# The GLA gate matmul of a hybrid decoder layer: two token halves in two 32-row groups of the array

## The reference, cut to what matters

```python
z = xn @ p["w_in"] + p["b_in"]               # all mixers' inputs, split by columns
# GLA, T = 528 tokens, 4 heads, GLA_DK = 128
g = jax.nn.log_sigmoid((a_lr @ p["w_gla_a2"] + p["b_gla_a"]).astype(jnp.float32)) / GLA_TAU
g = g.reshape(B, T, GLA_H, GLA_DK)
# per chunk of 64 tokens:
G = jnp.cumsum(g, axis=2)
decay = jnp.exp(jnp.where(causal[None, None, :, :, None], G[:, :, :, None, :] - G[:, :, None, :, :], -jnp.inf))
A = jnp.einsum("bhtk,bhtsk,bhsk->bhts", q, decay, k)
o = jnp.einsum("bhtk,bhkv->bhtv", q * jnp.exp(G), S) + jnp.einsum("bhts,bhsv->bhtv", A, v)
# afterwards
mix = sigmoid(gate_a) * y_a + sigmoid(gate_b) * y_b + sigmoid(gate_c) * y_c
h = h + rms_norm(mix @ p["w_out"], p["g_post_mix"])
```

## Time and profile before

| | us |
|---|---|
| median of 3 timed runs | 1294.49 (1294.04 to 1294.63) |
| the profiled execution's own time | 1293.61 |
| its span, first to last instruction | 1291.9 |
| mean granted TensorE clock | 0.999 |

### The profile page before, as it was taken

The page is one execution under the profiler, slowest core; times in us unless marked ns, Lnnn a source line. Parts: engine busy times, 40 slices in busy tenths (PEclk is TensorE's granted clock), DMA queues, the critical chain, the costliest instruction groups (busy, mean ns, idle before and its releaser), DMA issues.

```text
span 1291.9 us, 17528 instructions
## 1 busy us (share of the span) xinstructions
PE 1280.8 (99%) x6604; PEld 1042.3 (81%) x6604; DVE 602.7 (47%) x1086; ACT 398.0 (31%) x822; POOL 768.2 (59%) x919
## 2 busy tenths in 40 slices
PE   9999999999999999999999999999999999999998
PEld 8866887677898889777898987787888888888886
DVE  4248788642275766734545563241611111333434
ACT  5243555533013323434032334311511111212322
POOL 8737430125654543656864446786576676788882
PEclk9999999999999999999999999999999999999999
DMA  7745200223321222222343333443233333222221
GB/s 193 229 153 172 81 2 26 67 65 91 98 76 56 66 58 58 66 82 66 99 105 91 82 99 98 143 135 96 63 103 92 89 97 114 87 93 98 98 82 66
DMA packets 168445, 120.59 MB, mean 93 GB/s; under 512 B 12394, under 2 KB 146640, under 8 KB 168361
## 3 DMA queue, kind: packets, MB, share of 16 engines
q1 hardware_dynamic: 161654, 108.32, 28.9%
q10 hardware_dynamic: 6706, 11.15, 2.7%
HBM read 115.20 MB, written 9.62 MB: 97 GB/s over the span
## 4 chain that ended last, share of the span: by engine, by line
PE 98%; DVE 1%; ACT 1%; issue 0%; ACTq 0%
PE GP L1827 45%; PE GP L1862 9%; PE PA L1862 9%; PE GP L1842 7%; PE GP L1824 7%; PE PA L2026 3%; PE GP L2088 3%; PE PA L2230 2%; PE PA L2125 2%; PE PA L2063 1%; PE PA L2137 1%; PE GP L1907 1%; PE PA L1996 1%; PE PA L2222 1%; PE GP L2301 1%; PE PA L2027 1%
## 5 line engine op out<-in xcount | busy, mean ns | idle before, releaser
L622 POOL TENSOR_TENSOR wlo<-wraw,whi 128x256 fp32r<-128x256 f32 x712 | 566.1, 826 | 14.8
L618 POOL TENSOR_SCALAR whi<-wraw 128x1024 fp32r<-128x1024 f32 x178 | 194.9, 1095 | 484.0 <-PE GP L1827 248.6
L1827 PE MATMUL GP<-xh,whi 128*128 128x512 f32 x352 | 147.1, 418 | 0.0
L1827 PE MATMUL GP<-xh,wlo 128*128 128x512 f32 x352 | 139.1, 395 | 0.0
L1827 PE MATMUL GP<-xl,whi 128*128 128x512 f32 x352 | 138.8, 394 | 0.0
L1770 DVE TENSOR_TENSOR ul<-U,uh 128x512 fp32r<-128x512 f32 x64 | 65.0, 1051 | 109.7 <-ACT uh L1152 109.7
L1827 PE MATMUL GP<-nh,whi 128*128 128x512 f32 x240 | 95.1, 396 | 0.0
L1827 PE MATMUL GP<-nl,whi 128*128 128x512 f32 x240 | 95.1, 396 | 0.0
L1827 PE MATMUL GP<-nh,wlo 128*128 128x512 f32 x240 | 95.1, 396 | 0.0
L1774 DVE SCALAR_TENSOR_TENSOR U<-GP,rrow 128x512 f32<-128x512 f32 x32 | 22.1, 692 | 141.7 <-PE GP L1827 140.3
L1827 PEld LDWEIGHTS GP<-xh,whi 128*128 128x128 f32 x352 | 66.2, 188 | 17.3 <-issue 2.9
(11 more groups left out here) (406 smaller groups left out, 2789.9 us busy)
## 6 DMA issues: line engine op xcount, KB each, us to landing
wraw<-in_w_in SPq DMA_DIRECT2D x75, 512.0 KB, 3.8
wraw<-in_w_up SPq DMA_DIRECT2D x32, 512.0 KB, 4.0
wraw<-in_w_down SPq DMA_DIRECT2D x32, 512.0 KB, 3.5
line_rows<-bias_line SPq DMA_DIRECT2D x8, 655.0 KB, 5.2
table<-line_rows SPq DMA_DIRECT2D x4, 1024.0 KB, 5.2
wraw<-in_w_br_dsa SPq DMA_DIRECT2D x8, 512.0 KB, 4.0
wraw<-in_w_br_gla SPq DMA_DIRECT2D x8, 512.0 KB, 3.9
wraw<-in_w_br_ml SPq DMA_DIRECT2D x8, 512.0 KB, 4.1
```

The lines of the kernel that those rows point to most:

```text
L618: nc.gpsimd.tensor_scalar(hi, src, 1.0, 1.0, ALU.mult, ALU.mult).then_inc(hi_done, 1)
L622: part = nc.gpsimd.tensor_tensor(lo[:, at:to], src[:, at:to], hi[:, at:to].bitcast(FP32), ALU.subtract)
L1827: ins = mm(ps[0:t.m, 0:SEQ], wt[:, s0, w], av, start=st, stop=sp_)
```

## The change

The gate's product of each head is still two multiplies over 264 tokens each, but each now uses 32 rows of the array instead of 128: the first half of the tokens (b = 0) on partitions 32 to 63, the second (b = 1) on partitions 0 to 31. For that

- a second DMA puts the weight on partitions 0 to 15 of `a2` as well (L838 of the changed kernel), and the three DMAs raise `ld_a` to 48 instead of 32;
- DVE copies the second half of the gate rows (32 partitions x 264) from partitions 32 to 63 of `small` down to partitions 0 to 31 (L1375), after it has waited for `gla_c` = 1, and counts up `gla_c` to 2;
- PE waits, before `gq0`, for `ld_a` = 48 and for `gla_c` = 2.

```diff
@@ ACT @@
             act.wait_ge(a2_zero, 1)
-            act.dma_start(a2[32:32 + META, :], a["w_gla_a2"][0]).then_inc(ld_a, 16)
+            for r in (2 * META, 0):
+                act.dma_start(a2[r:r + META, :], a["w_gla_a2"][0]).then_inc(ld_a, 16)
@@ DVE @@
             nc.vector.memset(KHt[:, :], 0.0).then_inc(gla_c, 1)
             dve.wait_ge(gla_c, 1)
-            dve.wait_ge(ld_a, 32)
+            nc.vector.tensor_copy(small[0:2 * META, HALF:ALL], small[2 * META:4 * META, HALF:ALL]).then_inc(gla_c, 1)
+            dve.wait_ge(ld_a, 48)
@@ PE, gemm() @@
                     for b in range(2):
-                        ins = mm(ps[:, b * SEQ:b * SEQ + HALF], a2[:, h * DK:(h + 1) * DK], small[:, b * HALF:(b + 1) * HALF],
+                        r = slice(2 * META * (1 - b), 2 * META * (2 - b))
+                        ins = mm(ps[:, b * SEQ:b * SEQ + HALF], a2[r, h * DK:(h + 1) * DK], small[r, b * HALF:(b + 1) * HALF],
                                  start=True, stop=True)
@@ PE, between yb7 and gq0 @@
-            pe.wait_ge(ld_a, 32)
+            pe.wait_ge(ld_a, 48)
+            pe.wait_ge(gla_c, 2)
```

## The result

| | before | changed |
|---|---|---|
| median of the runs, us | 1294.49 | 1301.62 (1300.86 to 1302.01, 4 runs) |
| profiled execution's own time | 1293.61 | 1301.98 |
| its span | 1291.9 | 1300.2 |
| mean granted clock | 0.999 | 0.997 |

The ratio is 1.0055, with a 95% interval of 1.0039 to 1.0071: 7.1 us slower (5.0 to 9.2). The kernel is slower by more than its measurement is uncertain.

The account below looks back on a forecast made before the run. The prediction took PE to bound the kernel: wait +6.0, clock +1.5 and gates -0.8 make +6.7 us, so 1301.2 on the median of 1294.49. The range holding 8 in 10 was 1299.0 to 1303.4.

Parts of the forecast that it names:

- What bounds the kernel: PE, busy 1280.8 of 1291.9 us, sets the end; no slack there can absorb a delay at 341 us.
- The third rival: Later waits of PE shrink by as much as the delay at `gq0`, giving 1293.7 us; chance 0.03.
- The wait: Before `gq0`, PE waits for DVE's COPY behind five MEMSETs: start 5.93 us later, term +6.0 us (5.7 to 6.5).
- The straight line through two copies: DVE's COPY of 264 elements, interpolated between copies of 32 (0.18 us) and 384 (0.54): 0.42 us.
- The 0.1 on top: At `gq0`, first weights can't load while an earlier multiply runs: 0.1 us more in the wait's term.
- The clock: After the pause before `gq0`, PE runs at half pace for 3.4 us: +1.5 us (0 to 3.1).
- The first rival: The clock stays up through the pause before `gq0`: +5.2 us in all, 1299.7 us; chance 0.12.
- The gates: Gate products of four heads run as overlapping pairs: 0.27 us saved for `gg0`, 0.17 each for three others, -0.8 us.
- The second rival: The row groups of the gate products don't overlap: gates +0.8 us, time 1302.8 us; chance 0.08.
- The sum: Wait, clock and gates over the whole kernel: 6.0 + 1.5 - 0.8 = +6.7 us, 1301.2 on the median.

Follow-up runs that it names:

- e5: The changed kernel with DVE's COPY moved ahead of the five MEMSETs, right behind the product with `yb7`: 1297.07 us, ratio 1.0018.
- e2: The kernel before with only a wait added: PE waits for the last of the five MEMSETs before `gq0`: 1301.45 us, ratio 1.0055.
- e7: The changed kernel with 25 small multiplies on PE ahead of the wait, to fill it: 1299.74 us, ratio 1.0045.
- e4: The kernel before with both gate multiplies of a head on the same 32 rows, no copy and no new wait: 1296.76 us, ratio 1.0018.
- e6: The changed kernel with DVE's COPY between the third and fourth of the five MEMSETs: 1299.69 us, ratio 1.0047.
- e3: The changed kernel with 50 small multiplies on PE ahead of the wait: 1306.11 us, ratio 1.0091.
- e9: The kernel of e5 with nine small multiplies where PE waits ahead of the MLP: 1295.67 us, ratio 1.0011 against the kernel before.

## Why the prediction was right

**What bounds the kernel: right.** PE's list is the time, and a delay on PE at 341 us was not given back: the stages add up to the span's difference (8.31 of 8.3). The third rival (the wait is given back) is out.

**The wait: right, a little too long.** Forecast 5.93 to the start of `gq0`, measured 5.82. The COPY took 0.28 and not 0.42, and from its end to `gq0` it was 0.10 (346.88 to 346.98) and not 0.05. The straight line through two copies gave half too much because the earlier trace rows mix a copy made beside a working POOL (the one of 384 elements) with copies made while it was idle: the same COPY took 0.28 here, while POOL was idle, and 0.53 in e5, ahead of the MEMSETs, with POOL at work. That it is POOL which makes the difference fits all nine runs that have the COPY, but no run isolates it:

```profile
342.15 0.53 DVE L1369 COPY small<-small 32x264 f32<-32x264 f32 x1
```

The 0.1 on top, for `gq0`'s first weight load, is there, but behind the start of `gq0`: its second multiply comes 0.31 after the first in e5, at full clock (342.78 and 343.09), and 0.57 instead of 0.42 in the change.

**The clock: the step is right, the size was too small for this execution.** Forecast 1.5, from 3.4 us at half pace; measured 2.75 in the profiled execution (5.87 us at half pace, each losing 0.45), 1.73 in e2's, 1.9 by medians (e7 against the change). The range of 0 to 3.1 held it. Its price per microsecond, 0.45, was right: 2.6 of 2.75. The length was taken from a row that doesn't show the clock: PE's pace at the start was half, but the earlier trace rows have the granted clock at 1.00 there. The first rival (the clock stays up) is out by the windows of the change. e7 shows what such a kernel takes, 1299.74; that the rival's time, 1299.7, agrees so closely is in part luck, as its wait was 0.2 too long and its gates' gain 0.5 too large.

**The gates: the sign is right, the size is not.** Forecast -0.8, measured -0.26. The step that failed is "0.75 instead of 1.02, a gain of 0.27 for `gg0`". In the trace of before, the product behind `gg0` already waits for DVE's evacuation of the keys (L1391 there); this row of PE's weight loads, which the prediction didn't look up, says so:

```profile
353.54 0.19 PEld L1842 LDWEIGHTS GP<-whi,xh 128*128 128x128 f32 x1 [0.39 <-DVE kh L1391]
```

The evacuation doesn't depend on `gg0`, and behind a shorter `gg0` PE only waits longer for it: 0.22 us of PE's own wait now. From the last pair of `gk0`'s multiplies to `gv0A` it is 353.54 - 352.28 = 1.26 before and 362.17 - 360.91 = 1.26 after: no gain. For the other heads I had said 0.17 each. The timeline of before around `gg1`:

```profile
378.19 1.00 PE L2125 MATMUL PA<-QL,KL 128*128 128x64 f32 x8
379.02 1.11 PE L1847 MATMUL GP<-small,a 128*128 128x264 f32 x4
379.97 1.00 PE L2125 MATMUL PA<-QL,KL 128*128 128x64 f32 x8
```

The gate itself went from 0.95 (to the start of the next group) to 0.64, a gain of 0.31. But the first group before it takes 0.93 instead of 0.83, so from level group to level group it is 1.57 instead of 1.78, and the second group grew from 1.00 to 1.10. Its first weight load started 0.22 ahead of its first multiply before, and starts with it in the changed kernel:

```profile
379.75 1.08 PEld L2125 LDWEIGHTS PA<-QL,KL 128*128 128x128 f32 x8
```

```profile
388.38 0.97 PEld L2129 LDWEIGHTS PA<-QL,KL 128*128 128x128 f32 x8 [0.34 <-issue]
```

That leaves 0.1 net, and three times 0.1 is about the 0.26. The second rival, no overlap, is out: e4 shows what that looks like. Its remark that 32-row groups appear nowhere in the trace was a misreading: L1896 has four such multiplies at 9.6 to 10.6 us, 32 rows by 16 columns.

The Trainium skill's rule in "TensorEngine Tiling (Array Packing)", section "Tiling Modes", that a change of mode drains the engine, agrees with e4: with the drain and no overlap the gates lose 1.17 us. Its rule in "TensorE: Matmul & The Clock Gate", section "Why this matters for your kernels", to avoid idle gaps, agrees with e2 and e7.

**The sum.** 6.0 + 1.5 - 0.8 = 6.7 was forecast, 5.8 + 2.75 - 0.26 = 8.3 was measured in the profiled execution and 7.1 by medians. The errors of the clock and the gates add up in one direction and that of the wait goes against them. So the mechanism was right, but that 1301.2 came within 0.4 of the median of 1301.62 is in part luck: the clock's share is smaller in the medians than in the profiled execution, and the executions alone differ by more than that. The range's upper end doesn't follow from its terms, 1294.49 + 6.4 + 3.1 - 0.8 = 1303.2 and not 1303.4; nothing hangs on it.

## What to carry to other kernels

Before a wait is added on the engine that sets the end, list what stands in front of the signal on the other engine's queue: here a copy of 0.28 us cost 5.8, because five MEMSETs that nobody waited for stood ahead of it, and moving it up 48 us made it free. Price a pause of PE at more than its length, since the clock can fall in it. And a block on PE gains only if the next one is free to start: look at who ends the wait of the instruction behind it.

## What the runs showed that I had not expected

- The clock can fall after PE has gone on: in e6 PE restarted at 345.84 and the clock was still at 1.00 up to 346.40 and 0.50 from 346.55.
- Waits as short as 1.4 and 0.5 us, with 0.66 us of transposes between them, were followed by a fall in the profiled executions of e4 and e5 (the rows at 931 and 930 us) and of e3 (at 940), and not in those of the other kernels that have them, before and the change among them. Ahead of the first wait stand more transposes, so in e5 PE did nothing but eight instructions of transposes from 926.76 to 929.92. From the first multiply of the up projection to the first of the down projection e5 took 1109.54 - 923.82 = 185.72 us and e9, with the waits filled, 1108.57 - 924.25 = 184.32; the median went down by 1.4, too. So an edit with a small effect of its own can seem to cost more by a fall of the clock elsewhere: e4's stage grew by 1.17 and its median moved by 2.4. What decides whether the clock falls there is not shown; that PE reaches the pause at another time is a guess.
- A change of array mode costs time at both ends: a gate block on 32 rows without overlap lost about 0.3 us (e4), and with its pair side by side kept 0.1 of the 0.31 by which the block itself got shorter.
